# Keeping one block of expert rows on chip instead of two before a mixture-of-experts sum

## The reference, cut to what matters

```python
w = w / w.sum(-1, keepdims=True) * ROUTED_SCALE
routed = _grouped_experts(xt, idx, w, wg, wu, wd)     # 8 rows for each token, weighted and summed
xp = _layernorm(ALPHA * xp + mp[5] * (routed + _swiglu(xt, sg, su, sd)), ln2_g[l], ln2_b[l])
```

## Time and profile before

| | |
|---|---|
| median of 3 runs | 1741.38 us (1738.28 to 1743.87) |
| profiled execution, its own time | 1748.69 us |
| its span, first to last instruction | 1746.8 us |
| PE, DVE, ACT, POOL busy | 89%, 34%, 20%, 15% |
| DMA, mean over the span | 336 GB/s |
| expert blocks, first layer | about 320 to 888 us |
| combine, first layer | about 888 to 937 us |
| expert blocks, second layer | about 1128 to 1700 us |
| combine, second layer | about 1700 to 1744 us |

### The profile page before, as it was taken

The page is one execution under the profiler, slowest core; times in us unless marked ns, Lnnn a source line. Parts: engine busy times, 40 slices in busy tenths (PEclk is TensorE's granted clock), DMA queues, the critical chain, the costliest instruction groups (busy, mean ns, idle before and its releaser), DMA issues. The chain is left out here.

```text
span 1746.8 us, 19238 instructions
## 1 busy us (share of the span) xinstructions
PE 1548.8 (89%) x6878; PEld 744.8 (43%) x6878; DVE 597.9 (34%) x1424; ACT 356.1 (20%) x770; POOL 260.7 (15%) x229
## 2 busy tenths in 40 slices
PE   4899889897799899999887989898699989899887
PEld 1566644542344344344335744533243434344333
DVE  3233685532123111111148773632133111111117
ACT  3224621111111111111114272211011111111120
POOL 0010121111011123111104100111111122211100
PEclk9999999999899999999998989999899999999999
DMA  9890388599999999999994015689999999999994
GB/s 383 343 359 27 135 340 348 214 418 421 392 412 420 410 375 412 395 416 418 368 404 151 12 45 225 268 343 421 412 383 421 411 397 376 402 409 411 390 366 184
DMA packets 112499, 586.76 MB, mean 336 GB/s; under 512 B 22154, under 2 KB 24618, under 8 KB 54160
## 3 DMA queue, kind: packets, MB, share of 16 engines
q1 hardware_dynamic: 89264, 533.84, 75.5%
q0 software_dynamic: 22560, 50.00, 7.5%
q10 hardware_dynamic: 576, 1.66, 0.3%
HBM read 570.99 MB, written 45.30 MB: 353 GB/s over the span
## 5 line engine op out<-in xcount | busy, mean ns | idle before, releaser
L2990 DVE TENSOR_TENSOR scratch<-scratch,bank 128x256 f32<-128x256 f32 x84 | 51.5, 613 | 584.8 <-ACT scratch L2958 556.3
L2865 PE MATMUL bank<-weights,scratch 128*64 128x512 f32 x384 | 183.0, 631 | 45.8 <-DMA scratch<-in_moe_w_up 41.6
L2865 PE MATMUL bank<-scratch 128*64 128x512 f32 x352 | 168.0, 632 | 37.9 <-DMA weights<-in_moe_w_up 24.8
L2866 PE MATMUL bank<-scratch 128*64 128x512 f32 x384 | 186.6, 642 | 0.0
L2866 PE MATMUL bank<-weights,scratch 128*64 128x512 f32 x384 | 181.8, 627 | 0.0
L2958 ACT ACTIVATE scratch<-bank 128x256 f32<-128x256 f32 x84 | 32.2, 383 | 644.0 <-PE bank L2866 424.8
L2865 PEld LDWEIGHTS bank<-weights,scratch 128*64 128x64 f32 x384 | 53.8, 145 | 161.6 <-issue 161.3
L2865 PEld LDWEIGHTS bank<-scratch 128*64 128x64 f32 x352 | 49.6, 145 | 144.3 <-issue 144.1
L2595 POOL DMA_INDIRECT y_rows<-hP,y_idx x39 | 41.5, 1063 | 448.4 <-ACT hP L2966 330.5
L2580 POOL DMA_INDIRECT hP<-h_rows,tok_idx x78 | 81.3, 1043 | 135.4 <-PE bank L2541 61.7
L2871 PE MATMUL bank<-weights,scratch 128*128 128x512 f32 x224 | 98.6, 593 | 2.7 <-DMA weights<-in_moe_w_up 2.7
(11 more groups left out here) (400 smaller groups left out, 2445.9 us busy)
## 6 DMA issues: line engine op xcount, KB each, us to landing
weights<-in_moe_w_gate SPq DMA_DIRECT2D x62, 1024.0 KB, 12.8
weights<-in_moe_w_up SPq DMA_DIRECT2D x62, 1024.0 KB, 20.1
weights<-in_moe_w_down SPq DMA_DIRECT2D x62, 1024.0 KB, 21.3
scratch<-in_moe_w_gate SPq DMA_DIRECT2D x60, 1024.0 KB, 12.6
scratch<-in_moe_w_up SPq DMA_DIRECT2D x60, 1024.0 KB, 21.8
scratch<-in_moe_w_down SPq DMA_DIRECT2D x60, 1024.0 KB, 21.4
weights<-in_w_mod SPq DMA_DIRECT2D x6, 2048.0 KB, 11.4
wmod_more<-in_w_mod SPq DMA_DIRECT2D x6, 2048.0 KB, 8.6
```

Source lines behind the costliest of these rows:

```text
L2865: nc.tensor.matmul(out[0:HALF, :], x[:, 0:HALF], w0[:, kk], start=(kk == 0), stop=(kk == KT - 1))
L2866: m = nc.tensor.matmul(out[HALF:P, :], x[:, HALF:P], w1[:, kk], start=(kk == 0), stop=(kk == KT - 1))
L2990: nc.vector.tensor_tensor(B.h[b % 2].rearrange("p (j q) -> p q j", j=2), B.ex[b % 2].rearrange("p (q j) -> p q j", j=2), k.ps[2 + b % 2][: ...
```

## The change

The number of placed blocks goes from two to one. `y_placed` is written for any number.

```diff
-PLACED = 2
+PLACED = 1
...
-    y_placed = (B.y[(BLOCKS - 2) % 2], B.y[(BLOCKS - 1) % 2])
+    y_placed = [B.y[g % 2] for g in range(BLOCKS - PLACED, BLOCKS)]
```

## The result

The changed kernel is slower, by about two thirds of the forecast amount. Its median is 1753.38 us over 6 runs (1744.46 to 1756.63), against 1742.62 us over the 6 runs of the kernel before that it was compared with. The ratio is 1.005 with a 95% interval of 1.0032 to 1.0067, that is 5.6 to 11.7 us slower, 8.7 in the middle. The forecast was +13.2 us, 1754.6.

What follows compares the result with a forecast made beforehand. The weight stream was taken to bound the expert blocks, and part 3's landing plus 25.6 us of DVE each layer's end. The terms 5.3 + 7.8 + 1.4 - 1.3 gave +13.2 us, 1754.6 us; range 1747.5 to 1768 us.

Steps and rivals of the forecast that it cites:

- What bounds the end of a layer: In the combine, a layer ends at the landing of part 3 of the table plus 25.6 us of DVE.
- The wait as cause: At the seam, table reads wait for block 37's scatter; first reads go out 11.4 and 15.2 us later.
- Copy to scatter: On POOL at each layer's seam, 0.75 us from the end of block 37's copy to the scatter's start.
- Scatter to first read: At the seam, landing plus signalling: 7.0 us in the first layer, 5.5 in the second, near the gather.
- rival A: At the seam, the scatter stays as slow as under load, 8.9 and 9.7 us: +19.4, 1760.8 us; chance 0.24.
- Read to part 3: In the combine, first read to part 3 landed: 4 x 4.93 plus 4.5 us of start and lag, 24.2 us.
- Rival B: In the table reads, one engine again some 10 us behind: +26.7, 1768.1 us; sign: part 0 over 14 us; chance 0.13.
- So part 3: In the combine, part 3 lands 5.3 us later in the first layer, 7.8 us later in the second.
- Slowed PE: In the combine, PE idles and products after a pause are slower: 0.7 us on each layer, +1.4 us.
- Fill: In the first layer's weight stream, one fill of 0.52 MB removed: -1.3 us, bounds -1.3 and 0.
- Placed products and placing steps: Removing 5.2 us of PE in each combine and hidden DVE instructions beside the weight stream gains nothing on the path.
- Rival D: PE, not the table, ends the combine, so removing placed products pays: -11.7, 1729.7 us; chance 0.02.

Runs made afterwards that it cites:

- e2_scatter_waited: Kernel before plus one scatter of block 37's rows per layer to a spare table, the first table read waiting for its landing: 1749.67 us, ratio 1.0049.
- e1_scatter_only: Kernel before plus the spare scatter ahead of the read signal on POOL, its landing awaited only at the combine's end: 1745.74 us, ratio 1.0013.
- e3_placed_none: Changed kernel with no block placed, no fill, reads waiting for the very last block's scatter: 1757.45 us, ratio 1.0086 to the kernel before.
- e7_fills: Kernel before with four more fills in the first layer, beside routed blocks 14 to 17, 2.1 MB more: 1746.67 us, ratio 1.0.
- e10_tiles: Kernel before with PE's placed products taken tile by tile, each just ahead of that tile's rows: 1757.36 us, ratio 1.0084.
- e6_tables_late: Kernel before with the norm's tables issued behind part 3 of the reads instead of ahead of all: 1736.91 us, ratio 0.9961.
- e8_after_tables_late: Changed kernel with the norm's tables issued behind part 3 of the reads: 1756.07 us, ratio 1.0064 to the kernel before.
- e5_scatter_behind: Kernel before plus the spare scatter in each layer, issued behind the read signal and awaited at the very end: 1746.58 us, ratio 1.0017.
- e12_warm_again: Changed kernel plus nine filler products on PE per layer before part 0, second run: 1752.09 us, ratio 1.005 to the kernel before.

## Why the prediction was right

**What bounds the end of a layer: right.** From DVE's start on part 3 (912.51 and 1723.05) to its last scaling it took 25.65 and 24.75 us, against 24.46 and 24.33 before; the waits of 1.10 and 0.32 us for PE are nearly all of the difference. But for them, delays of part 3 came out one to one.

**The wait as cause: right, and shown** by `e2_scatter_waited`, which has the scatter and the wait and nothing else of the change (its wait in the first layer was 1.3 us longer), against `e1_scatter_only`, which has the scatter without the wait for its landing, and by the profile of `e3_placed_none`.

**Copy to scatter, 0.75 us:** 0.76 in both layers.

**Scatter to first read, 7.0 and 5.5 us:** 5.5 and 4.4. The landing took 5.0 and 3.9 us by the DMA issues of the changed kernel:

```profile
y_rows<-z,y_idx POOLq DMA_INDIRECT x1, 5.0
y_rows<-z,y_idx POOLq DMA_INDIRECT x1, 3.9
```

In the quiet second layer the gather, 4.1 us, was the right neighbour to 0.2 us, and I should have stayed at it; rival A, which took the loaded scatter, is out.

**Read to part 3, 24.2 us:** 22.4 and 22.5. The 4.93 us for each part were right (the three from part 0 to part 3 took 14.8 and 15.0 us); the start took 2.6 to 2.7 us, not the 4.5 of the cold weights. Rival B, that the lag returns, is out: DVE began part 0 7.65 and 7.49 us after its issue, far from 14.

**So part 3:** +2.0 and +5.1 us against the last copy, where I had +5.3 and +7.8. These two terms are what was mis-sized, by 6.0 us together.

**Slowed PE, +1.4 us:** 1.4 of waiting in one profile, 0 in the other, and no gain from the filler products. **Fill, -1.3 us:** 0 (`e7_fills`). **Placed products and placing steps, nothing on the path:** right so far as `e2_scatter_waited`, which keeps them all, loses as much as the changed kernel within the intervals. `e10_tiles` shows the same from the other side: they lie in PE's waits.

**Rival D:** PE does not end the combine in the kernel before, and a PE made later there (`e10_tiles`) costs at once, so its margin is thin. With the tables moved it does hold DVE. The rival's condition was real, one edit away.

The sum from the profile is 3.2 + 5.5 = 8.7 us; the ratios gave 8.7 and 7.8; the medians 10.8. The forecast of 13.2 lies above the first interval's 11.7. The mechanism was the one forecast; the two mis-sized terms erred the same way, and the two small ones, the fill and the slowed PE, had no support and cancelled each other by luck.

**What stays open.** Why some DMA engines are late in the kernel before (that they are is inferred from the 34 GB/s of the earlier trace rows; no view shows them one by one). The tables were part of it (`e6_tables_late`); what was left, part 0 landing 11.2 and 12.6 us after its issue, was only argued to be weights. Why two scatters beside the reads cost some 3 us, if they do (0.7 to 5.2), is not settled either; and the reason why in `e1_scatter_only` the second layer's read went out 3.5 us behind a scatter whose landing it did not wait for, the profile does not name.

## What to carry to other kernels

A write to memory and its read back is a chain of its own: price it as copy, issue, landing, signal and cold start of the read, and look for what else the transfer queue had to do in that time. Here the reads were sent 10 and 14 us later and the end came 3 and 6 us later, because they had stood behind a backlog; the same look showed the better change, to move what stands ahead of them, where such a backlog is. Work that ran in an engine's unavoidable wait was free here, and putting it "nearer to its use" put it on the path.

## What the runs showed of the hardware

- An indirect scatter of 128 rows of 4 KB landed in 3.9 and 5.0 us in windows that moved 50 to 112 GB/s in all, its own bytes among them; in such a gap it took 2.6 us (`e8_after_tables_late`, first layer) to 6.1 us (`e2_scatter_waited`, first layer). Beside a full stream it took 8.4, and 10.4 and 10.1 us beside the reads of the table (`e5_scatter_behind`).
- In the changed kernel the burst of reads after the gap delivered its first 2.1 MB after 7.5 to 7.6 us and then each 2.1 MB in 4.9 to 5.0. In one other profile of the same burst DVE got its first part only 9.2 us after the issue (`e12_warm_again`, first layer).
- The Trainium skill (DMA: Bandwidth & Descriptors, Latency and other measured facts) puts the slower engines down, as a guess, to rings that scatters and gathers use. The lag of the kernel before was there and went with an idle queue; scatters ran in both kernels, so no run here shows that cause.
